# Step attention: a head's differences and weights ahead of the samples' clamp and exponent, and the first chunk ahead of the weights at the turns

## The reference

```
z = q.k / sqrt(64) + bias_h
log_keep = log_sigmoid(-z)   where key < query, else 0
excl     = sum of log_keep over later keys
weights  = exp(log_sigmoid(z) + excl)   where key < query, else 0
out      = weights @ v        (12 heads of 64)
```

## Time and profile before

| | |
|---|---|
| median of 3 runs | 1889.07 us (1888.73 to 1897.35) |
| profiled execution, own time | 1890.35 us |
| its span | 1888.4 us |
| PE busy | 1784.3 us (94%) |
| PEld (weight loads) busy | 1644.7 us (87%) |
| DVE busy | 1016.3 us (54%) |
| ACT busy | 726.8 us (38%) |
| POOL busy | 327.7 us (17%) |
| mean granted clock of TensorE | 0.98 of full speed |

### The profile page before, as it was taken

How to read it: one execution, slowest core, us unless ns; L and a number is a source line. 1 busy time by engine, 2 the same in 40 slices (tenths; PEclk the granted TensorE clock), 3 DMA queues, 4 the chain that set the end, 5 groups by cost and what they waited for, 6 DMA issues and landing times. The chain is left out here.

```text
span 1888.4 us, 36341 instructions
## 1 busy us (share of the span) xinstructions
PE 1784.3 (94%) x13404; PEld 1644.7 (87%) x13404; DVE 1016.3 (54%) x1848; ACT 726.8 (38%) x1245; POOL 327.7 (17%) x452
## 2 busy tenths in 40 slices
PE   8999899999699999999999999799899999999997
PEld 6999688898498999999998998455588999998997
DVE  3663455552427676666226434565535777768224
ACT  4343333331445333335226113454446333336222
POOL 1554344452001222221000000000000222221000
PEclk9999999998799999999999999899999999999999
DMA  4222111100422222223221216778711222222222
GB/s 170 72 84 78 69 35 34 33 20 21 169 78 68 78 87 79 78 89 106 89 89 65 82 67 258 241 260 267 244 58 54 89 78 88 83 84 76 100 86 87
DMA packets 90655, 188.60 MB, mean 100 GB/s; under 512 B 9442, under 2 KB 41570, under 8 KB 90194
## 3 DMA queue, kind: packets, MB, share of 16 engines
q1 hardware_dynamic: 90050, 185.26, 29.2%
q0 software_dynamic: 528, 2.32, 0.3%
HBM read 176.00 MB, written 11.55 MB: 99 GB/s over the span
## 5 line engine op out<-in xcount | busy, mean ns | idle before, releaser
L673 PE MATMUL PB<-parts,wparts 128*128 128x288 f32 x8664 | 1165.9, 297 | 22.8 <-DVE wparts L642 11.5
L673 PEld LDWEIGHTS PB<-parts,wparts 128*128 128x128 f32 x8664 | 1160.0, 190 | 27.2 <-DVE wparts L642 21.7
L632 ACT ACTIVATE wparts<-ring 128x1024 fp32r<-128x1024 f32 x198 | 209.9, 1060 | 680.0 <-PE PB L673 677.1
L642 DVE TENSOR_TENSOR wparts<-ring,wparts 128x1024 fp32r<-128x1024 f32 x174 | 212.8, 1224 | 270.0 <-ACT wparts L632 260.4
L1032 POOL COPY cnew<-arena 128x2 f32 (+1 forms) x106 | 113.0, 1066 | 340.0 <-DVE arena L957 337.2
L969 DVE SCALAR_TENSOR_TENSOR arena<-arena,ffw 128x512 f32<-128x512 f32 x176 | 133.7, 760 | 19.3 <-DVE arena L970 12.8
L683 PE MATMUL PB<-parts,wparts 128*128 128x288 f32 x648 | 104.8, 310 | 4.5 <-DVE parts L514 3.3
L954 DVE TENSOR_TENSOR arena<-PB,rstd_in 128x288 f32<-128x288 f32 x88 | 40.1, 456 | 121.8 <-PE PB L673 115.2
L683 PEld LDWEIGHTS PB<-parts,wparts 128*128 128x128 f32 x648 | 91.0, 188 | 14.0 <-DVE parts L514 7.3
L1008 DVE SCALAR_TENSOR_TENSOR arena<-arena,dnw 128x512 f32<-128x512 f32 x54 | 58.1, 1075 | 32.8 <-ACT arena L907 27.6
L931 ACT ACTIVATE arena<-arena,ffw 128x512 f32<-128x512 f32 x88 | 63.8, 725 | 27.4 <-issue 15.5
(11 more groups left out here) (309 smaller groups left out, 2076.5 us busy)
## 6 DMA issues: line engine op xcount, KB each, us to landing
ring<-in_w SPq DMA_DIRECT2D x198, 512.0 KB, 3.2
arena<-in_kpages SPq DMA_DIRECT2D x64, 256.0 KB, 5.2
arena<-in_vpages SPq DMA_DIRECT2D x64, 256.0 KB, 4.8
arena<-in_kpages SPq DMA_DIRECT2D x64, 128.0 KB, 2.3
arena<-in_vpages SPq DMA_DIRECT2D x64, 128.0 KB, 2.3
membuf<-in_w SPq DMA_DIRECT2D x8, 512.0 KB, 5.7
arena<-in_state_dn SPq DMA_DIRECT2D x6, 512.0 KB, 5.1
o_dns_s<-arena SPq DMA_DIRECT2D x6, 512.0 KB, 3.9
```

Of the source, the lines that this page charges most:

```text
L632: nc.scalar.activation(wparts[:, 0, k, :], ring[:, k, :], ACT.Copy).then_inc(hi_ready, 1)
L642: nc.vector.tensor_tensor(wparts[:, 1, k, :], ring[:, k, :], wparts[:, 0, k, :].bitcast(F32), ALU.subtract).then_inc(lo_ready, 1)
L673: last = nc.tensor.matmul(dst(b), wparts[:, part, k, block * P:(block + 1) * P], x[:, row_, b * HALF:(b + 1) * HALF], start=start and part ...
```

## The change

In `act_turn`, with a following layer, the high part and the square of chunk 0 (first half) are issued ahead of the wait for `unit_done` and the split of the weight tile; the later loop starts from chunk 1. In `act_sb` a head's weights are issued ahead of the next set's Exp and Ln, and in `dve_sb` a head's differences ahead of the next set's mask and clamp. For even heads and for head 11, which have no such set step in that place, the order is what it was.

```diff
--- before.py
+++ after.py
@@ -562,6 +562,8 @@
             act_squares(act, post, k, 1, 0)
             act_post(act, post, 0)
             act_scaled(act, post, k, 1, dst, 0).then_inc(half_out, 1)
+            if then:
+                act_pre(act, then, post, 0, 0)
             act.wait_ge(unit_done, end - 1)
             if then:
                 act_hi(act, name, 0, 0, UNITS[name])
@@ -581,7 +583,7 @@
                 late_scaled()
                 return
             norm = PRE[then]
-            for c in range(KD):
+            for c in range(1, KD):
                 act_pre(act, then, post, 0, c)
                 if c == 2:
                     late_squares()
@@ -2044,11 +2046,11 @@
             st["act"].skip(act, -1, "o1")
             for h in range(SB_H):
                 k, more = h // 2, h // 2 + 1 < SETS
+                act_head_w(act, h)
                 if h % 2 and more:
                     act_set_s(act, k + 1)
                 elif h % 2:
                     st["act"].skip(act, k, "xe", "xl")
-                act_head_w(act, h)
                 if h % 2 == 0:
                     act_set_t(act, k)
                     if k:
@@ -2148,9 +2150,9 @@
             dve_set_d(dve, 0)
             for h in range(SB_H):
                 k, more = h // 2, h // 2 + 1 < SETS
+                dve_head_d(dve, h)
                 if h % 2 and more:
                     dve_set_k(dve, k + 1)
-                dve_head_d(dve, h)
                 if h % 2 == 0:
                     dve_set_t(dve, k)
                 elif more:
```

## The result

| | before | changed |
|---|---|---|
| median, six runs each | 1890.39 us (1888.18 to 1897.35) | 1909.65 us (1896.75 to 1912.03) |
| ratio | | 1.0083, 95% interval 1.0065 to 1.0101 |
| span of the profiled execution | 1888.4 us | 1908.2 us |
| median in later runs | 1891.02 to 1893.15 us (23 to 30 runs) | 1908.59 us (6 runs), ratio 1.0086 (1.0070 to 1.0103) |

The change costs 0.8 to 0.9%, some 16 us. The forecast was slower by 10.6 us, with 1905 us as its upper end. Forecast and result have the same sign; the size was too small.

What follows compares the result with a forecast made beforehand. TensorE is busy 94% of the span, but the VectorE and ScalarE chain paces the odd attention legs. Terms: 9.75 + 7.0 - 5.1 - 1.0 = +10.6 us, giving 1899.7 us; range 1892 to 1905 us.

Steps and rivals of the forecast that it cites:

- That nothing is gained by going first: Odd heads: differences and weights never waited for the samples' work, so putting them first brings nothing.
- The odd legs: Odd to next even head: samples' Ln ends later, delaying their maximum and the next head's bias; 5 x 1.95 = +9.75 us.
- The clock: Ahead of heads 2, 4, 6, 8, 10: about 3.4 us TensorE idle halves the clock; +7.0 us, bounds 0 and 8.5.
- The page waits: Ahead of heads 5 and 7: page waits and head 7's slow clock are absorbed; -5.1 us, bounds 0 and -5.1.
- B: Rival on attention's page loads: they slip with TensorE, so 5.1 us stay; +15.7 us, 1904.8 us; chance 0.13.
- The turns: Into up0, k, up1: first chunk ahead of the weights' copy; 2 x -0.55 and +0.06 us, together -1.0 us.
- The base: Whole kernel: the forecast difference is added to the median of three runs, 1889.07 us; profiled span 1888.4 us.
- Rival A: Ahead of even heads: the clock holds, legs cost +3.6 us in all, 1892.7 us; chance 0.2.
- The rule named with it: TensorE idle ahead of even heads: a strict reading of its idle gap leaves the clock up, without the 7.0 us.
- C: Rival: the page stream paces the whole attention and the longer odd legs vanish; -6.1 us, 1883.0 us; chance 0.05.
- D: Rival: the three turns pay 0.77 us each for the late copy; +13.9 us, 1903.0 us; chance 0.05.

Runs made afterwards that it cites:

- after_late: Changed kernel with the set's maximum behind the next head's bias and clamp, and the scan behind that head's maximum, on VectorE; ratio 1.0013 (0.9999 to 1.0028).
- attn_only: Kernel before with only the attention's order changed (`act_sb` and `dve_sb`), the turns being the old ones; ratio 1.0103 (1.0085 to 1.0122).
- act_only: Kernel before with only ScalarE's attention order changed: a head's weights ahead of the set's Exp and Ln; ratio 1.0084 (1.0051 to 1.0117).
- fill_turns: Kernel before with the changed turns and extra TensorE products, results unused, in four idle times; median 1888.24 us, ratio 0.9979 (0.9964 to 0.9995).
- after_filler: Changed kernel with two extra 512-column products, results unused, in TensorE's idle time ahead of each even head; ratio 1.0006 (0.9989 to 1.0024).
- dve_only: Kernel before with only VectorE's attention order changed: a head's differences ahead of the set's clamp; ratio 1.0021 (1.0000 to 1.0041).
- zfirst_turns: Kernel before with the changed turns and, on TensorE, an even head's scores ahead of the set's first half product with V; ratio 1.0009 (0.9993 to 1.0026).
- fill_turns_zfirst: As fill_turns, and on TensorE an even head's scores ahead of the first half of the set's product with V; ratio 0.9980 (0.9963 to 0.9998).

## Why the prediction was off

- **That nothing is gained by going first:** right. The weights start at 5.10 us behind the sums in both kernels.
- **The odd legs:** mechanism right (the samples' Ln behind the weights, L2121 late, L2094 behind it), and after_late shows it by taking only that away. The size was 1.95 us and is 1.71 us; L2094 does start 1.85 us late, but takes 0.14 us less.
- **The clock:** the step that failed is the price of the falls, in "a fall ahead of heads 2, 4, 6, 8 and 10 and price each at the mean, 1.4 us". The falls came, four in the changed kernel (none ahead of head 2) and five in attn_only and act_only, and most cost 3.0 us: the clock stayed at 0.50 for 6.8 us and not for 3.4 us. The four cost 10.7 us where the sum had 7.0 us for five. Why some last 3.4 us and others 6.8 us stays open. Its bound of 5 x 1.7 us was too low as well, for both rows under it had a short fall. I also left out that head 11's fall may grow; it did, by 1.3 us. With the runs' numbers: 8.6 + 10.7 + 1.3 - 5.2 - 1.0 = +14.4 us, against the 16 us of the ratios (interval 12 to 19 us).
- **The page waits:** right for this kernel, all absorbed (none at L1876 behind set 1), and B falls. That a change of timing can open others, for V pages, the prediction doesn't consider; after_late and fill_turns show it.
- **The turns:** right to 0.1 us in the traces (-0.55 and -0.6 us into up1 and up0, +0.06 us into k); the timed runs can't tell them from nothing.
- **The base:** the profile of before had up1 at 130.0 ns a matmul, which no other profile here has in that stage, and its median of three was 1889.07 us where 30 runs give 1893.15 us.
- **Rival A** (the clock holds) is what after_filler realises by other means. The rule named with it, from the Trainium skill (TensorE: Matmul & The Clock Gate, HAM oscillation — how this bites in real kernels), puts the limit too high for this kernel, and the measurement decides: dve_only had 2.2 to 2.5 us of idle and a fall at four of five even heads. Its picture of a fall at the same wait in every tile is what attn_only and act_only show; the changed kernel shows it at four of five. C and D had no part.

## What to carry to other kernels

An operation that waits for another engine holds up everything behind it in its own queue. Before moving work to a later place, look for the operation that waits for its result, and for what stands behind that one. Where the wait makes TensorE idle, price the clock with it: here a loss of 1.7 us became 4.7 us at heads 6, 8 and 10, and two products whose results nobody uses took the other 3.0 us back.

## Not expected of the hardware

- A fall of the clock behind 3.2 us of idle lasted 3.4 us or 6.8 us: 1.7 or 3.0 us of the path. At head 2 of the changed kernel it didn't come, in either profile. Behind 2.2 to 2.5 us it came at four of five places (dve_only), behind 1.48 us (before) and 1.28 us (after_filler) at none. The length of one idle time doesn't settle it: in zfirst_turns, at 1270 us, a fall began within a wait of 1.56 us, with 1.1 us of work between it and a wait of 1.09 us; in fill_turns_zfirst two waits of 0.77 and 1.51 us with the same work between them had no fall behind them.
- At a granted clock of 1.00 TensorE spaces the same matmuls of 288 columns at 133.3 ns or at 130.0 ns, for hundreds of us on end. In the first profile of before the spacing was 133 ns at the start of up1 and 130.0 ns from the end of a short fall of the clock on. What chooses it was not tried.
